# An encoder layer in fp32 on one core: another order at the two heads of the second feed-forward part, norm sums by eight products of ones, norm factors of phase one in PSUM

## The chip, the cores and the metric

The kernel runs on one core of one Trainium2 chip. The metric is the time of one launch in device microseconds (us), the median of several runs; lower is better. The engines are TensorE (PE; its weight loads are PEld), VectorE (DVE), ScalarE (ACT) and GpSimd (POOL); SyncE (SP) issues the DMAs. Each engine works through its own list of instructions in program order, and semaphores tie the lists together.

## The reference

One layer over 1024 + 512 = 1536 token columns with D = 1024, in fp32: a feed-forward part, a mixing part with two kinds of attention heads, a second feed-forward part, a norm at the end. The change touches the end of the mixing part and the second feed-forward part:

```python
def rmsnorm(x, g):
    y = xf * lax.rsqrt(jnp.mean(xf * xf, axis=-1, keepdims=True) + EPS)
    return (y * g).astype(x.dtype)

def swiglu(h, wg, wu, wd):
    return (jax.nn.silu(h @ wg) * (h @ wu)) @ wd
...
x = x + g2 * token_mixing(h, ...)              # ends in  concat(oa, ob) @ w_out
h = modulate(rmsnorm(x, ffn2_norm), sh3, sc3)  # h * (1 + sc3) + sh3
x = x + 0.5 * g3 * swiglu(h, ffn2_wg, ffn2_wu, ffn2_wd)   # D_FF = 2816
x = rmsnorm(x, final_norm)
```

## The kernel before

**Three products for one.** Weights and activations are split into a high and a low half; a product is three products on PE (`three_pass`). ACT copies the high half of a weight tile (`W_hi`), POOL subtracts it from the tile and so makes the low half (`W_lo`). W_hi and W_lo have three slots (WS).

**Output projection** (`wo_*`, L2092 to L2210). The columns are cut into NWC = 4 chunks of NB = 384, and each of the 32 steps (chunk c, row block m) multiplies 8 k-blocks by 3 products, 24 in all, into one of the PSUM banks 0 to 3; DVE adds the result to the state `XT`. The sum of squares over the 1024 rows, which the norm of the next part wants, is made per chunk: ACT squares 8 row blocks (`sums_act`, L737), four slots at a time; POOL adds them in pairs (`pair_up`, L755); PE multiplies each pair sum by a matrix of ones into bank 6 (`sums_pe`, L767), two products (a half, at m = 7) and later two more (at m = 3 of the next chunk). A product of fp32 operands with ones stands in the trace as two matmuls. Then ACT takes the root (`root_act`), DVE the reciprocal (`root_dve`): the norm factor, kept in `rstd_a` (chunks 0, 1: phase one) and `rstd_b` (chunks 2, 3: phase two). The pair sums of chunk 3 are not made before the second part has begun.

**Second feed-forward part** (`st_*`, L2332 to L2712). It works in two phases h = 0, 1 of 768 columns each, with NR = 11 rounds per phase, so 22 rounds R (round 0 is the first of phase one, round 11 the first of phase two; rounds 10 and 21 are each phase's last). A round makes the gate and up products of 256 hidden rows by a scheme of seven products instead of eight for a 2 x 2 block product: PN = 7 products with the names B11, B21, T1, T2, T3, T4, B22, made in this order (`st_product`, L2647), each of 24 matmuls. Then 16 steps of the down product (`st_down`, L2676), 6 matmuls each. The seven weight units and the two down tiles of a round are units u = 0 to 8. Their sources are four quarters of the weights (`quart`), of which POOL makes sums and differences in place (`st_sum`, no = 0 to 3; unit 2 is `qsum`).

**The operands of the seven products** are the normed activations and their differences. Per phase and operand: DVE multiplies state, gain and norm factor (`op_x_dve`, L2279; four row blocks, in one or two pieces), ACT adds the shift (`op_shift_act`), DVE makes the differences T1 to T4 (`op_t_dve`), ACT copies the high half (`op_hi_act`), DVE subtracts for the low part (`op_lo_dve`). For phase one this stands in the projection's last two chunks and the head of round 0; for phase two in rounds 10 and 11.

**Inside a round** ACT copies products out of PSUM (`part_keep_act`), DVE adds them to the next ones (`st_add_dve`), ACT and DVE make the hidden values in four pieces (`st_silu_act`, `st_hidden_dve`, `st_hid_act`, n = 0 to 3). The down product's step 6 waits for the last hidden piece; its steps from the ninth on wait for the additions into the state (`st_down_dve`), of which DVE must have done all but seven. ACT's first split of the next round, `st_hi_act(R, 0, 1)`, stands at the end of its round. SP loads two quarters for the next round behind unit 5's low half and two behind unit 8's.

The order of all this is written out by hand, one function per engine: `st_act` (L2505), `st_dve` (L2598), `st_pool` (L2439), `st_pe` (L2703), and `wo_act`, `wo_pool`, `wo_pe`, `wo_dve` for the projection.

## Time and profile before

| | |
|---|---|
| median of 3 runs | 3147.92 us (3145.74 to 3148.78) |
| the profiled execution | 3152.61 us, its span 3150.7 us, mean granted clock 0.983 |
| busy, whole span | PE 3020.5 us (96%), DVE 1667.9, POOL 1361.6, ACT 1193.6 |
| in the chain that ended last | PE 40%, POOL 9% (of it 8% in attention), issue 6%, DVE 4%, ACT 2% |
| output projection | about 1940 to 2076 us |
| second feed-forward part | 2076 to about 3136 us, then the final norm |

How to read it: the profile is of one execution; a line number is that of the kernel. In a timeline a row is a start, a duration (of the whole group, where it says x2 or more), the engine, line and operation, output<-input, and in brackets the engine's idle time before it with what ended it. The granted clock is a share of PE's full clock: 1.00 is 2.4 GHz, 0.50 is 1.2 GHz.

### The profile page before, as it was taken

The numbers are of one execution on the slowest core, as the hardware profiler recorded it, in microseconds if no ns is written. First come the engines' busy times: TensorE is split into PE (matmuls) and PEld (weight loads), VectorE is DVE, ScalarE is ACT, GpSimd is POOL, SyncE is SP. The second block draws the span as 40 slices with busy tenths as digits, with TensorE's granted clock in tenths as the row PEclk, the third lists the DMA queues.
The fourth block names the chain that finished last, engine by engine and source line by source line (L and its number), as shares of the span: only waits on it lengthen the run. The fifth ranks groups of instructions, "written<-read, shape, count | busy, mean of one in ns | idle before, by whom it ended". The sixth has DMA issues, their size and how long they took to land.

```text
span 3150.7 us, 45626 instructions
## 1 busy us (share of the span) xinstructions
PE 3020.5 (96%) x15385; PEld 2608.0 (83%) x15385; DVE 1667.9 (53%) x3010; ACT 1193.6 (38%) x2026; POOL 1361.6 (43%) x765
## 2 busy tenths in 40 slices
PE   7999999999999988997989999989999998999998
PEld 3888888888888867885656667979999998999998
DVE  5576667766672346886544332353433456434435
ACT  6311111111111135775767775443333343333334
POOL 0111111111111143333646666666666666666673
PEclk9999999999999999998999999989999999999999
DMA  7121212212121023556413225422222121222222
GB/s 268 39 69 52 65 55 80 68 52 63 57 75 34 27 81 119 146 141 163 121 54 83 74 77 160 119 74 67 67 80 67 60 74 41 81 67 67 67 80 100
DMA packets 341520, 262.50 MB, mean 83 GB/s; under 512 B 19771, under 2 KB 309934, under 8 KB 341422
## 3 DMA queue, kind: packets, MB, share of 16 engines
q1 hardware_dynamic: 341422, 261.21, 28.2%
q8 instruction: 59, 0.97, 0.1%
q14 instruction: 39, 0.32, 0.0%
HBM read 215.71 MB, written 45.45 MB: 83 GB/s over the span
## 4 chain that ended last, share of the span: by engine, by line
PE 40%; POOL 9%; issue 6%; DVE 4%; ACT 2%; SPq 1%; DMA 0%; DVEq 0%; POOLq 0%; ACTq 0%
POOL XT_r L1967 8%; PE PS L2671 6%; PE PS L2672 6%; PE PS L2673 6%; PE PS L518 6%; PE PS L519 6%; PE PS L520 6%; POOL W_lo L2416 0%; DVE SL L2327 0%; PE PS L1666 0%; DVE XT L2177 0%; ACT SLf L2303 0%; PE PS L772 0%; ACT z_sb L1184 0%; POOL W_lo L2116 0%
## 5 line engine op out<-in xcount | busy, mean ns | idle before, releaser
L512 POOL TENSOR_TENSOR W_lo<-raw,W_hi 128x1024 fp32r<-128x1024 f32 x66 | 158.7, 2411 | 959.0 <-ACT W_hi L480 959.0
L518 PE MATMUL PS<-H_hi,W_hi 128*128 128x512 f32 (+1 forms) x1312 | 500.3, 381 | 1.9 <-DVE H_lo L1921 1.4
L519 PE MATMUL PS<-H_lo,W_hi 128*128 128x512 f32 (+1 forms) x1312 | 497.0, 379 | 0.0
L520 PE MATMUL PS<-H_hi,W_lo 128*128 128x512 f32 (+1 forms) x1312 | 496.9, 379 | 0.0
L2416 POOL TENSOR_TENSOR W_lo<-quart,W_hi 128x1024 fp32r<-128x1024 f32 x132 | 320.4, 2436 | 263.5 <-ACT W_hi L2412 263.5
L2671 PE MATMUL PS<-SL,W_hi 128*128 128x384 f32 x1056 | 356.6, 338 | 20.8 <-POOL W_lo L2416 19.8
L1967 POOL TENSOR_TENSOR XT_r<-XT,XT_r 128x512 fp32r<-128x512 f32 x224 | 287.0, 1287 | 181.7 <-ACT XT_r L1819 181.1
L2672 PE MATMUL PS<-SL,W_hi 128*128 128x384 f32 x1056 | 355.4, 337 | 0.0
L2673 PE MATMUL PS<-SL,W_lo 128*128 128x384 f32 x1056 | 355.0, 336 | 0.0
L2177 DVE SCALAR_TENSOR_TENSOR XT<-PS,mod,XT 128x384 f32<-128x384 f32 (+1 forms) x480 | 243.2, 534 | 186.2 <-PE PS L520 186.2
L480 ACT ACTIVATE W_hi<-raw 128x1024 fp32r<-128x1024 f32 x66 | 68.6, 1055 | 604.2 <-PE PS L520 604.2
L496 DVE SCALAR_TENSOR_TENSOR ada_acc<-ada_r,silu_c,ada_acc 128x128 f32<-128x128 f32 x672 | 290.4, 473 | 11.9
L518 PEld LDWEIGHTS PS<-H_hi,W_hi 128*128 128x128 f32 x1312 | 246.8, 188 | 45.1 <-DVE H_lo L1921 1.6
L2412 ACT ACTIVATE W_hi<-quart 128x1024 fp32r<-128x1024 f32 x132 | 139.7, 1059 | 376.5 <-PE PS L520 252.1
L519 PEld LDWEIGHTS PS<-H_lo,W_hi 128*128 128x128 f32 x1312 | 246.9, 188 | 41.4
L520 PEld LDWEIGHTS PS<-H_hi,W_lo 128*128 128x128 f32 x1312 | 246.7, 188 | 41.5
L680 DVE SCALAR_TENSOR_TENSOR XT<-PS,mod,XT 128x512 f32<-128x512 f32 x264 | 197.3, 749 | 155.7 <-PE PS L520 155.6
L518 PE MATMUL PS<-hid,W_hi 128*128 128x384 f32 x704 | 237.4, 337 | 6.1 <-POOL W_lo L2416 5.3
L519 PE MATMUL PS<-hid,W_hi 128*128 128x384 f32 x704 | 236.3, 336 | 0.0
L520 PE MATMUL PS<-hid,W_lo 128*128 128x384 f32 x704 | 236.3, 336 | 0.0
L2671 PEld LDWEIGHTS PS<-SL,W_hi 128*128 128x128 f32 x1056 | 200.3, 190 | 22.9 <-POOL W_lo L2416 21.1
L518 PE MATMUL PS<-hid_hi,W_hi 128*128 128x512 f32 x528 | 209.3, 396 | 5.5 <-DVE XT L680 4.9
(294 smaller groups left out, 6291.0 us busy)
## 6 DMA issues: line engine op xcount, KB each, us to landing
ada_r<-in_ada_w SPq DMA_DIRECT2D x192, 128.0 KB, 2.3
quart<-in_ffn_wg SPq DMA_DIRECT2D x88, 256.0 KB, 3.9
quart<-in_ffn_wu SPq DMA_DIRECT2D x88, 256.0 KB, 4.1
down<-in_ffn_wd SPq DMA_DIRECT2D x44, 512.0 KB, 3.5
raw<-in_w_out SPq DMA_DIRECT2D x30, 512.0 KB, 3.7
ada_w_sb<-in_ada_w SPq DMA_DIRECT2D x6, 2048.0 KB, 15.8
raw<-in_ffn_wg SPq DMA_DIRECT2D x22, 512.0 KB, 4.1
raw<-in_ffn_wu SPq DMA_DIRECT2D x22, 512.0 KB, 4.5
```

What stands on the lines that cost most here:

```text
L496: mm = dve.scalar_tensor_tensor(out=acc_, in0=w, scalar=c, in1=acc_, op0=ALU.mult, op1=ALU.add)
L512: pool.tensor_tensor(W_lo[:, n % WS, :], raw[:, n % RS, :], W_hi[:, n % WS, :].bitcast(F32), ALU.subtract).then_inc(w_ready, 1)
L518: pe.matmul(out, w_hi, m_hi, start=first, stop=False)
L519: pe.matmul(out, w_hi, m_lo, start=False, stop=False)
L520: return pe.matmul(out, w_lo, m_hi, start=False, stop=last)
L680: dve.scalar_tensor_tensor(out=xt, in0=PS[:, 6 + i % DS, :], scalar=hgate[:, g, m, c:c + 1], in1=xt, op0=ALU.mult, op1=ALU.add).then_inc(a ...
L1967: pool.tensor_tensor(p_lo(i), e_slot(i), p_hi(i).bitcast(F32), ALU.subtract).then_inc(p_lo_done, 1)
L2177: mm = dve.scalar_tensor_tensor(out=xt, in0=PS[:, bank, a - c * NB:b - c * NB], scalar=hgate[:, g, m, s:s + 1], in1=xt, op0=ALU.mult, op1= ...
L2416: pool.tensor_tensor(W_lo[:, st_slot(u), :], unit_src(u), W_hi[:, st_slot(u), :].bitcast(F32), ALU.subtract) \
L2671: pe.matmul(out, w_hi, m_hi, start=j in PRODUCT_OPENS and kp == 0, stop=False, skip_group_check=True)
L2672: pe.matmul(out, w_hi, m_lo, start=False, stop=False, skip_group_check=True)
L2673: mm = pe.matmul(out, w_lo, m_hi, start=False, stop=kp == 3, skip_group_check=True)
```

## The change

It has three parts. First, the norm sums before the second feed-forward part (b = 2) multiply each of the eight squares by ones, where they multiplied four pair sums; POOL's pair adds are gone, 12 in the projection and 4 in round 0. Second, the norm factors of phase one (chunks 0 and 1) are kept in PSUM banks 4 and 5, not in SBUF (`rstd_a`). Third, the hand-written orders at the heads of both phases change: ACT splits the first three weight units before the operand copies T3, T4, B22; POOL makes unit 2's low half before the difference no = 2; the sums of chunk 3 stand behind T2 and T3, not behind B21 and T1; its root and reciprocals later. For phase two, B11's multiplies and shifts go from round 10 into round 0 (in a free home of their own, rows 12 to 15 of the chunk named EDGE), its high and low copies into the first half of round 10, and the other operands are reordered in rounds 10 and 11, with the first split of round 11 in front of hidden piece 3.

The diff, context cut:

```diff
                 c = i - 2 * NCH
-                return (rstd_a, rstd_b)[c // 2][:, c % 2, :]
+                return PS[:, 4 + c, 0:NB] if c < 2 else rstd_b[:, c % 2, :]
             return rstd_m[:, c * CH:(c + 1) * CH] if i // NCH == 1 else rstd[:, c, :]
...
             for p in range(NPP) if half is None else range(2 * half, 2 * half + 2):
+                if b == 2:
+                    pe.wait_ge(sq_ready, i * KD + 2 * p + 2)
+                    pe.matmul(sum_bank(b), ones[:, :], sq_slot(i, 2 * p), start=(p == 0), stop=False)
+                    pe.matmul(sum_bank(b), ones[:, :], sq_slot(i, 2 * p + 1), start=False,
+                              stop=(p == NPP - 1)).then_inc(sq_used, 1)
+                    continue
                 pe.wait_ge(sq_paired, i * NPP + p + 1)
...
                 wo_split_lo(pool, i)
-                if i % KD == 6 and i // KD < NWC - 1:
-                    pair_up(pool, 2, i // KD, 0)
-                if i % KD == 2 and i > KD:
-                    pair_up(pool, 2, i // KD - 1, 1)
 
...
         RAW_NO = {B11: 0, B21: 4, B12: 8, B22: 13}
-        SHIFT_NO = {B11: 0, B21: 4, B12: 8, B22: 12}
+        SHIFT_NO = ({B11: 0, B21: 4, B12: 8, B22: 12}, {B11: 0, B12: 4, B22: 8, B21: 12})
         OP_T = {T1: (T3, B11), T2: (B22, T1), T4: (B21, T2), T3: (B22, T3)}
...
 
-        def raw_row(j, kp):
+        EDGE = NWC - 1
+        def raw_row(h, j, kp):
             kb, nb = RAW_AT[j]
-            return SLf[:, KD * kb + 4 + kp, nb, :]
+            return SLf[:, 12 + kp, EDGE, :] if h == 1 and j == B11 else SLf[:, KD * kb + 4 + kp, nb, :]
+        def raw4(h, j):
+            return SLf[:, 12:16, EDGE, :] if h == 1 and j == B11 else operand4(SLf, X4f, j, 1)
 
...
             c = 2 * h + nb
-            dve.wait_ge(rstd_ready, 2 * NCH + (2 if h == 0 and nb == 0 else 3 if h == 0 else NWC + 1) - 1)
+            dve.wait_ge(rstd_ready, 2 * NCH + 2 * h + nb + 1)
             if h == 0:
                 dve.wait_ge(wo_done, (1 + nb) * KD)
+            elif j == B11:
+                dve.wait_ge(sq_used, 2 + (2 * NCH + NWC) * NPP)
             else:
...
                     cut = slice(a - c * NB, b - c * NB)
-                    mm = dve.scalar_tensor_tensor(out=raw_row(j, kp)[:, cut], in0=XT[:, k, a:b], scalar=hscale[:, 2, k, s:s + 1],
-                                                  in1=(rstd_a, rstd_b)[h][:, nb, cut], op0=ALU.mult, op1=ALU.mult)
+                    mm = dve.scalar_tensor_tensor(out=raw_row(h, j, kp)[:, cut], in0=XT[:, k, a:b], scalar=hscale[:, 2, k, s:s + 1],
+                                                  in1=(PS[:, 4 + nb, cut] if h == 0 else rstd_b[:, nb, cut]), op0=ALU.mult, op1=ALU.mult)
                 mm.then_inc(op_x, 1)
...
                 for a, b, s in column_spans(c * NB, (c + 1) * NB):
-                    row = raw_row(j, kp)[:, a - c * NB:b - c * NB]
+                    row = raw_row(h, j, kp)[:, a - c * NB:b - c * NB]
                     mm = act.activation(row, row, ACT.Identity, bias=mod[:, SH3 * KD + 4 * kb + kp, s:s + 1])
...
         def op_t_dve(dve, h, j):
-            dve.wait_ge(op_shift, h * 2 * KD + {T1: 12, T2: 16, T4: 16, T3: 16}[j])
+            dve.wait_ge(op_shift, h * 2 * KD + {T1: 12 - 4 * h, T2: 16 - 4 * h, T4: 16, T3: 16 - 4 * h}[j])
             if j != T1:
...
             a, b = OP_T[j]
-            dve.tensor_tensor(operand4(SLf, X4f, j, 1), operand4(SLf, X4f, a, 1), operand4(SLf, X4f, b, 1), ALU.subtract) \
+            dve.tensor_tensor(operand4(SLf, X4f, j, 1), raw4(h, a), raw4(h, b), ALU.subtract) \
                .then_inc(op_x, 1)
...
             else:
-                act.wait_ge(op_shift, h * 2 * KD + SHIFT_NO[j] + 4)
-            act.activation(operand4(SL, X4, j, 0), operand4(SLf, X4f, j, 1), ACT.Copy).then_inc(op_hi, 1)
+                act.wait_ge(op_shift, h * 2 * KD + SHIFT_NO[h][j] + 4)
+            if h == 1 and j == B11:
+                act.wait_ge(st_steps, st_at(NR - 1, product_step(B11, 1)))
+            act.activation(operand4(SL, X4, j, 0), raw4(h, j), ACT.Copy).then_inc(op_hi, 1)
 
         def op_lo_dve(dve, h, j):
-            dve.wait_ge(op_hi, OPH0 + h * PN + j + 1)
-            dve.tensor_tensor(operand4(SL, X4, j, 1), operand4(SLf, X4f, j, 1), operand4(SL, X4, j, 0).bitcast(F32), ALU.subtract) \
+            dve.wait_ge(op_hi, OPH0 + h * PN + (T1 if h == 1 and j == B21 else j) + 1)
+            dve.tensor_tensor(operand4(SL, X4, j, 1), raw4(h, j), operand4(SL, X4, j, 0).bitcast(F32), ALU.subtract) \
                .then_inc(op_ready, 1)
...
                     src = io["ffn2_wd"][0][bass.ds((R * 2 + (t - 2 * h * NR)) * P, P), :]
-                    sp.wait_ge(unit_ready, unit_at(R, 3 + t))
+                    sp.wait_ge(unit_ready, unit_at(R, 4 if is_round(R, 0) else 3 + t))
                     sp.dma_start((down0, down1)[t][:, :], src).then_inc(down_landed[t], 16)
...
             def body(R, h):
-                for u in (2,) if is_round(R, 0) else (1, 2):
-                    st_lo_pool(pool, R, u)
+                if not is_round(R, 0):
+                    st_lo_pool(pool, R, 1)
+                st_lo_pool(pool, R, 2)
                 if is_round(R, 0):
-                    pair_up(pool, 2, NWC - 1)
+                    st_sum(pool, 0, 2)
                 st_sum(pool, R, 3)
...
             st_lo_pool(pool, 0, 1)
-            for no in range(3):
+            for no in range(2):
                 st_sum(pool, 0, no)
...
         DOWN_BANKS = (6, 7, 0, 1, 2, 3, 4, 5)
-        EDGE = NWC - 1
         HOME_1, HOME_E = 8, 10
...
             def body(R, h):
+                turns = is_round(R, NR - 1)
                 if not is_round(R, 0):
                     st_hi_act(act, R, 1)
-                st_hi_act(act, R, 2)
+                    st_hi_act(act, R, 2)
                 if is_round(R, NR):
-                    for j in (T2, T3, T4, B22):
-                        op_hi_act(act, 1, j)
+                    op_hi_act(act, 1, T2)
                 part_keep_act(act, R, 0)
                 part_keep_act(act, R, 1)
+                if is_round(R, 0):
+                    op_hi_act(act, 0, T4)
                 st_hi_act(act, R, 3)
+                if is_round(R, NR):
+                    for j in (T3, T4, B22):
+                        op_hi_act(act, 1, j)
                 if is_round(R, 0):
+                    op_hi_act(act, 0, B22)
                     sums_act(act, 2, NWC - 1, (0, 4))
...
                     sums_act(act, 2, NWC - 1, (4, KD))
+                if turns:
+                    op_hi_act(act, 1, B11)
                 st_hi_act(act, R, 5)
-                if is_round(R, 0):
-                    root_act(act, 2, NWC - 1)
                 part_keep_act(act, R, 2)
                 part_keep_act(act, R, 3)
-                if is_round(R, NR - 1):
-                    op_shift_act(act, 1, B11)
                 st_hi_act(act, R, 6)
...
                 part_keep_act(act, R, 5)
-                if is_round(R, NR - 1):
-                    op_shift_act(act, 1, B21)
-                    op_hi_act(act, 1, B11)
+                if is_round(R, 0):
+                    root_act(act, 2, NWC - 1)
                 st_hi_act(act, R, 7)
...
                 st_silu_act(act, R, 2)
-                if is_round(R, NR - 1):
-                    op_shift_act(act, 1, B12)
                 st_hi_act(act, R, 8)
                 st_hid_act(act, R, 2)
-                if is_round(R, NR - 1):
-                    op_hi_act(act, 1, B21)
+                if turns:
+                    op_shift_act(act, 1, B12)
+                    st_hi_act(act, R, 0, 1)
                 st_silu_act(act, R, 3)
                 st_hid_act(act, R, 3)
-                if is_round(R, NR - 1):
+                if is_round(R, 0):
+                    op_shift_act(act, 1, B11)
+                if turns:
                     op_hi_act(act, 1, T1)
                     op_shift_act(act, 1, B22)
-                if not is_round(R, 2 * NR - 1):
+                    op_shift_act(act, 1, B21)
+                    op_hi_act(act, 1, B21)
+                elif not is_round(R, 2 * NR - 1):
                     st_hi_act(act, R, 0, 1)
 
-            st_hi_act(act, 0, 0)
+            for u in range(WS):
+                st_hi_act(act, 0, u)
             op_hi_act(act, 0, T3)
-            op_hi_act(act, 0, T4)
-            st_hi_act(act, 0, 1)
-            op_hi_act(act, 0, B22)
             st_rounds(act, body)
...
                 if turns:
-                    op_x_dve(dve, 1, B11)
+                    op_lo_dve(dve, 1, B11)
                     op_x_dve(dve, 1, B21)
-                if is_round(R, 0):
-                    root_dve(dve, 2, NWC - 2)
-                    root_dve(dve, 2, NWC - 1)
                 st_add_dve(dve, R, 1)
...
                 st_hidden_dve(dve, R, 1)
+                st_hidden_dve(dve, R, 2)
                 if turns:
                     op_x_dve(dve, 1, B12)
-                st_hidden_dve(dve, R, 2)
-                if turns:
-                    op_t_dve(dve, 1, T1)
                 st_add_dve(dve, R, 3)
...
                 if turns:
+                    op_t_dve(dve, 1, T1)
+                if is_round(R, 0):
+                    root_dve(dve, 2, NWC - 2)
+                    root_dve(dve, 2, NWC - 1)
+                if turns:
                     op_x_dve(dve, 1, B22)
...
                     st_down_dve(dve, R, h, i)
+                    if is_round(R, 0) and i == 7:
+                        op_x_dve(dve, 1, B11)
                     if turns:
                         if i == 3:
-                            op_lo_dve(dve, 1, B11)
-                        if i == 6:
                             op_t_dve(dve, 1, T2)
-                        if i == 9:
+                        if i == 7:
                             op_t_dve(dve, 1, T4)
-                        if i == 12:
+                        if i == 11:
                             op_lo_dve(dve, 1, B21)
...
                     st_product(pe, R, h, j)
-                    if is_round(R, 0) and j in (B21, T1):
-                        sums_pe(pe, 2, NWC - 1, j - B21)
+                    if is_round(R, 0) and j in (T2, T3):
+                        sums_pe(pe, 2, NWC - 1, j - T2)
                 st_down(pe, R, h)
...
```

Three places on ACT show the order. The first is the head of the second feed-forward part. `W_hi<-quart` and `W_hi<-qsum` are weight splits, `SL<-SLf` and `X<-X4f` high copies of operands, `SLf<-PS` copies of products, `SLf<-XT` squares. Before:

```order
L2412 ACTIVATE W_hi<-quart 128x1024
L2323 ACTIVATE SL<-SLf 128x4x384
L2323 ACTIVATE X<-X4f 128x1536
L2412 ACTIVATE W_hi<-quart 128x1024
L2323 ACTIVATE SL<-SLf 128x4x384
L2412 ACTIVATE W_hi<-qsum 128x1024
L2492 ACTIVATE SLf<-PS 128x384 x2
L2412 ACTIVATE W_hi<-quart 128x1024
```

After:

```order
L2423 ACTIVATE W_hi<-quart 128x1024 x2
L2423 ACTIVATE W_hi<-qsum 128x1024
L2334 ACTIVATE SL<-SLf 128x4x384
L2503 ACTIVATE SLf<-PS 128x384 x2
L2334 ACTIVATE X<-X4f 128x1536
L2423 ACTIVATE W_hi<-quart 128x1024
L2334 ACTIVATE SL<-SLf 128x4x384
L753 ACTIVATE SLf<-XT 128x384 x4
```

The three splits stand together now, ahead of the copies of T3 (first `SL<-SLf`), T4 (`X<-X4f`) and B22.

The second is ACT's list from the split of the last down tile to the end of round 0. Before:

```order
L2412 ACTIVATE W_hi<-down 128x1024
L2503 ACTIVATE hid<-PS 128x384
L2499 ACTIVATE hid_g<-PS 128x384
L2503 ACTIVATE hid<-PS 128x384
L2412 ACTIVATE W_hi<-quart 128x1024
```

After:

```order
L2423 ACTIVATE W_hi<-down 128x1024
L2514 ACTIVATE hid<-PS 128x384
L2510 ACTIVATE hid_g<-PS 128x384
L2514 ACTIVATE hid<-PS 128x384
L2312 ACTIVATE SLf<-SLf,mod 128x256
L2312 ACTIVATE SLf<-SLf,mod 128x128
...
L2423 ACTIVATE W_hi<-quart 128x1024
```

Eight shifts of phase two's B11 (four rows in pieces of 256 and 128 columns) have moved in front of round 1's first split.

The third is the end of round 10 and the start of round 11. Before:

```order
L2323 ACTIVATE SL<-SLf 128x4x384
L2303 ACTIVATE SLf<-SLf,mod 128x384 x4
L2412 ACTIVATE W_hi<-quart 128x1024 x2
L2412 ACTIVATE W_hi<-qsum 128x1024
L2323 ACTIVATE SL<-SLf 128x4x384 x2
L2323 ACTIVATE X<-X4f 128x1536
L2323 ACTIVATE SL<-SLf 128x4x384
L2492 ACTIVATE SLf<-PS 128x384 x2
L2412 ACTIVATE W_hi<-quart 128x1024 x2
L2499 ACTIVATE hid_g<-PS 128x384
```

After:

```order
L2334 ACTIVATE SL<-SLf 128x4x384
L2423 ACTIVATE W_hi<-quart 128x1024
L2423 ACTIVATE W_hi<-qsum 128x1024
L2334 ACTIVATE SL<-SLf 128x4x384
L2503 ACTIVATE SLf<-PS 128x384 x2
L2423 ACTIVATE W_hi<-quart 128x1024
L2334 ACTIVATE SL<-SLf 128x4x384
L2334 ACTIVATE X<-X4f 128x1536
L2334 ACTIVATE SL<-SLf 128x4x384
L2423 ACTIVATE W_hi<-quart 128x1024
L2510 ACTIVATE hid_g<-PS 128x384
```

The first split of round 11 has left this place (it stands further ahead, before hidden piece 3), T2's copy stands alone in front of the product copies, and the copies of T3, T4 and B22 behind the next split.

## Rows read from the trace of the kernel before

**Rows 1.** Windows: busy time per engine (instructions), granted clock, DMA share, GB/s.

```profile
1975.00:2025.00 50.00, 50.00 (x280) 48.40 (x279) 16.47 (x23) 21.26 (x29) 30.17 (x16) 1.00 0.36 106
...
2076.00:2123.00 47.00, 32.74 (x148) 30.05 (x147) 18.64 (x15) 22.67 (x31) 31.71 (x15) 0.82 0.16 49
2123.00:2169.00 46.00, 46.00 (x266) 45.72 (x265) 17.76 (x30) 16.23 (x25) 30.87 (x14) 1.00 0.24 70
```

**Rows 2.** PE's waits in the whole span: us in total, times, longest.

```profile
PE PS L2671 <- POOL W_lo L2416: 19.8, 3, 9.7
...
PE PS L518 <- POOL W_lo L2416: 5.3, 1, 5.3
```

**Rows 3.** Timeline of PE: start, us, operation, idle before it and its releaser.

```profile
2088.66 0.69 PE L2671 MATMUL PS<-SL,W_hi 128*128 128x384 f32 x1 [8.21 <-POOL W_lo L2416]
...
2099.26 0.56 PE L772 MATMUL PS<-SLf,ones 128*128 128x384 f32 x1 [4.08 <-POOL SLf L759]
...
2110.02 0.50 PE L2671 MATMUL PS<-SL,W_hi 128*128 128x384 f32 x1 [1.98 <-POOL W_lo L2416]
...
2592.60 0.66 PE L518 MATMUL PS<-hid,W_hi 128*128 128x384 f32 x1 [5.34 <-POOL W_lo L2416]
...
2635.71 0.69 PE L2671 MATMUL PS<-SL,W_hi 128*128 128x384 f32 x1 [9.65 <-POOL W_lo L2416]
```

**Rows 4.** Windows of 2 us, PE alone: busy (matmuls), granted clock.

```profile
2090.00:2092.00 2.00, 2.00 (x7) 0.50 0.00 0
```

**Rows 5.** Timeline of ACT: the split that waits for a round's last product.

```profile
2145.44 1.06 ACT L2412 ACTIVATE W_hi<-quart 128x1024 fp32r<-128x1024 f32 x1 [11.06 <-PE PS L520]
...
2557.36 1.06 ACT L2412 ACTIVATE W_hi<-quart 128x1024 fp32r<-128x1024 f32 x1 [12.14 <-PE PS L520]
...
2612.25 1.06 ACT L2412 ACTIVATE W_hi<-quart 128x1024 fp32r<-128x1024 f32 x1 [11.66 <-PE PS L520]
...
2670.97 1.06 ACT L2412 ACTIVATE W_hi<-quart 128x1024 fp32r<-128x1024 f32 x1 [12.28 <-PE PS L520]
```

**Rows 6.** Timeline of PE: starts of two following halves of products of ones.

```profile
2039.52 0.81 PE L772 MATMUL PS<-x_sqo,ones 128*128 128x384 f32 x2
...
2057.46 0.81 PE L772 MATMUL PS<-x_sqo,ones 128*128 128x384 f32 x2
```

**Rows 7.** Timeline of DVE: four multiplies by a norm factor, POOL busy and idle.

```profile
2055.70 4.33 DVE L2292 SCALAR_TENSOR_TENSOR SLf<-XT,mod,rstd_a 128x384 f32<-128x384 f32 x4
...
2596.75 2.20 DVE L2292 SCALAR_TENSOR_TENSOR SLf<-XT,mod,rstd_b 128x384 f32<-128x384 f32 x4
```

**Rows 8.** Timelines of POOL and DVE at the projection's end.

```profile
2063.96 7.57 POOL L2116 TENSOR_TENSOR W_lo<-raw,W_hi 128x1024 fp32r<-128x1024 f32 x2 [5.94 <-ACT W_hi L2112]
...
2065.49 3.78 DVE L2315 TENSOR_TENSOR X4f<-SLf 128x1536 f32<-128x1536 f32 x1
...
2069.72 7.30 DVE L2327 TENSOR_TENSOR SL<-SLf,SL 128x1536 fp32r<-128x1536 f32 x2
...
2083.00 1.74 DVE L2327 TENSOR_TENSOR X<-X4f,X 128x1536 fp32r<-128x1536 f32 x1
```

**Rows 9.** Timelines round the end of round 0, and multiplies for phase two.

```profile
2109.84 2.55 DVE L779 RECIPROCAL rstd_b<-rstd_b 128x384 f32<-128x384 f32 x1 [4.33 <-ACT rstd_b L764]
...
2125.99 2.40 POOL L2416 TENSOR_TENSOR W_lo<-down,W_hi 128x1024 fp32r<-128x1024 f32 x1 [1.87 <-ACT W_hi L2412]
...
2130.81 1.72 DVE L2177 SCALAR_TENSOR_TENSOR XT<-PS,mod,XT 128x384 f32<-128x384 f32 x3
...
2133.31 1.06 ACT L2412 ACTIVATE W_hi<-quart 128x1024 fp32r<-128x1024 f32 x1 [3.01 <-DMA quart<-in_ffn_wu]
...
2573.59 2.71 DVE L2292 SCALAR_TENSOR_TENSOR SLf<-XT,mod,rstd_b 128x256 f32<-128x256 f32 x8
```

**Rows 10.** Timelines of DVE and ACT in round 11.

```profile
2633.37 0.96 DVE L2567 TENSOR_TENSOR PS<-PS,SLf 128x768 f32<-128x768 f32 x1
...
2635.49 0.49 ACT L2503 ACTIVATE hid<-PS 128x384 fp32r<-128x384 f32 x1 [0.63 <-DVE PS L2587]
```


## The prediction

> **What bounds the kernel now.** I read the windows first: in the output projection (first row of [rows 1]) PE is busy 50.00 of 50 us at full clock, and so it is in an ordinary round. Only the stretch behind 2076 is thin: 32.74 of 47 us, mean clock 0.82. So PE sets the time, and the other engines count only where PE waits. The list of waits says for whom: POOL's low halves of weights, 19.8 us in three waits and 5.3 in one [rows 2]. PE's timeline places them [rows 3]: 8.21, 4.08 and 1.98 us in round 0 (the middle one for the pair adds), 5.34 and 9.65 in rounds 10 and 11. Behind each the clock is at its lower level for a while (0.50, so 1.2 GHz, 7 matmuls in 2 us where full clock has 12 [rows 4]), which costs some 2 us a time. ACT's first weight split of a round waits for PE's last product of the round before and marks the rounds [rows 5]: round 1 begins at 2145.4, round 10 at 2557.3 (45.8 us each), round 12 at 2670.9. Round 0 begins at 2076.0: 24 products at 0.173 us (46 us hold 266, [rows 1]) and 8.2 idle before 2088.66. So round 0 takes 69.4 us, where 45.8 and 2.6 for its norm sums would do: 21 too many. Rounds 10 and 11 take 113.6 against 91.5: 22 too many. These 43 us are all that an order can win.
>
> **Part one: eight products of ones.** Two logical products stand in the trace as x4. From one half's start to the next are 17.94 us [rows 6], and between them lie 96 weight products, 16.64 us; so a half costs 1.30. The change gives each half four instead of two: +1.30 for each of six halves in the output projection, where PE is never idle: +7.8 us on the path. POOL's pair adds that go there cost nothing (POOL waits for ACT, ACT for PE). The two halves of round 0 move and grow to 2.6 each; they are in the walk below.
>
> **Part two: norm factors in PSUM.** Four multiplies by a norm factor take 4.33 us while POOL works and 2.20 while it doesn't [rows 7]: the waiting one lets a POOL operation pass. The same holds for other DVE work with both inputs in SBUF [rows 8]: two splits on POOL take 7.57 us instead of 2 x 2.39, the subtraction between them on DVE 3.78 instead of 1.74, two more 7.30. The two engines take turns, one operation each. With the factor in PSUM one SBUF input is left, and 4.33 should become about 2.3. This is worth 0: the shift behind it on ACT waits for the root, and that for PE's sums. The Trainium skill ("SBUF — State Buffer", Who interferes with whom) says that a VectorE instruction with two SBUF inputs contends with a GpSimd one that reads SBUF, and that one with a single SBUF input doesn't; by this rule, the trace agrees. The same rule speaks against the next part, whose subtractions now stand where POOL has a queue.
>
> **Part three, round 0.** Times from the end of the projection (2076.0 before), each step a wait and a duration: split on ACT 1.06, on POOL 2.39, DVE subtraction 1.7, turns as above. Up to the first low half nothing changes its place: POOL ends it at -0.6, DVE then takes its turn (T1's low part) to 1.0, and the second low half is there at 3.4 instead of 12.6. B21 runs from 4.2 to 8.3, no wait: 8.2 saved. But POOL now has a sum, a difference and the third low half in a row, and DVE's operations take turns with them: T3's subtraction to 5.05, POOL's sum to 7.4, T2's low part to 9.05, the difference to 11.4, T3's low part (its copy comes off ACT at 9.9) to 13.05, the low half to 15.4. The product T1 waits 7.1 us for it. Then T4's low part to 17.05, two more differences to 21.8 and the fourth low half: T2 at 24.2 (before at 34.0, with 2.6 of sums in front). T2 runs at the lower clock to 30.4, sums to 33.0. The second four squares on ACT wait for these sums, and behind them on ACT stand a weight split and the copy of T2's product, for which T3 waits: squares to 33.9, split 35.0, copy 35.5. T3 starts 2.5 us late. Then T3, sums, T4, B22 at 4.16, 2.6, 4.16, 4.16 and about 2 for the clock: the down products start at 52.7. Before: 2145.4 less 16.6 is 2128.8, also 52.7. Worth 0, between -8 (POOL and DVE don't hinder each other: T1 at 9.0, T2 at 16.2, down at 44.7) and +2.
>
> **End of round 0.** From the start of the down products: DVE ends the hidden part at 2.1, then two reciprocals of 2.55 [rows 9] that stood earlier before, to 7.2, eight additions at 0.55 [rows 9] to 11.6, then the eight multiplies for phase two's B11, 2.7 to 3.3 with POOL waiting (2.71 in [rows 9]), to 14.9. ACT shifts the last at 15.6, and only then splits the first quarter of round 1: 16.7, where it did so at 4.5 before (2133.31 in [rows 9], waiting for its DMA). POOL's low half stands at 19.1, and PE wants it at 16.6: 2.5 late. Behind it on POOL are two sums and the next low half: 26.3, where B11 of round 1 ends at 23.3: 3.0 more. Round 1 loses 5.5; the lower clock behind the first gap stretches B11 inside the second. Bounds 3 and 8.
>
> **Rounds 10 and 11.** From round 10's start. B11's multiplies are gone from it, so DVE gives the sums for B22 at 23.6, PE needs them at 25.0; the last low half stands at 28.6, the down products start at 29.1 instead of 35.3: 5.9 saved. But DVE's multiplies for B12 start at 27.3 and let a POOL sum pass (to 33.2); the quarter for round 11 lands 4.9 us behind the last low half (2128.4 to 2133.3 in [rows 9]), at 33.5; ACT splits it to 34.8 and then does hidden 3, done at 37.0, which PE wants at 35.4: 1.7. Then DVE does T1's subtraction and B22's multiplies, and three POOL operations pass between them, to 45.8, before the first addition of the down products; PE stands at its ninth product from 39.1 to 46.4: 7.3. Eight more m's of 1.04 and 2 for the clock end the round at 57.0; before at 54.9 (2612.25 in [rows 5]). In round 11 the weight of T2 doesn't wait for four copies on ACT any more: T2 at 72.6 instead of 78.4. But DVE's addition in B21's banks stands behind five low parts and a subtraction, each with a turn of POOL's: at 79.9, before at 76.1 [rows 10]. Hidden 0 is through ACT 2.6 us behind the addition's start [rows 10], then come a split (1.06) and the copy of T2's product (0.49): 84.0. T3 waits for this copy. Before, T3 started at 84.6 (78.4, a product and 2 for the clock), the copies following PE at once. Worth 0, between -13 (no turns: 71) and +3.
>
> **Sum.** 7.8 + 0 + 5.5 + 0 = 13.3 us. The profiled execution took 3152.6, so 3165.9 by the profiler's run; it lies 4.7 above the median of 3147.9, so 3161 as median.
>
> **Rivals.** *It gains by part (a).* The order does what its words say and POOL and DVE hinder each other less than in rows 8, since the instructions meet at other moments: -8 in round 0, +5.5, -11 in rounds 10 and 11, +7.8: 6 us faster, 3142. For it: turns depend on arrivals within a microsecond. Against: in rows 8 each meeting costs a full operation. *It gains fully (b).* Every wait gone: -43 + 7.8 + 2.6, 3115. Against: four chains above would all have to be wrong. The other side of my forecast is (a): the point from which it decides is T1 in round 0 at 12 or earlier and T3 in round 11 at 75 or earlier. *Only the PE work counts (c).* The hold on round 1's first quarter is hidden, since DVE catches up sooner: 7.8 + 0 + 1, and 4 won in round 11 because T2 is earlier: 5 slower, 3153. Against: the hold is in ACT's program order, not in a race. *Slower still (d).* Turns also hit round 1 and T4, and clock losses add up: +20 to +24, 3170.
>
> **How the numbers follow.** Forecast 0.48, (a) 0.16, (b) 0.04, (c) 0.20, (d) 0.12. The likeliest case alone spans 3155 to 3168. The range for 8 in 10 reaches from just above (a), 3144, to 3171. A change below 0.2% (6.3 us) can't be told from none here. Faster by more: (b) and 0.10 of (a), 0.14. Same: 0.06 of (a), 0.14 of (c), 0.04 of the forecast: 0.24. Slower: 0.62.
>
> **What would show it.** x_sqo products 48 instead of 24, the projection 7.8 longer from its first to its last product. In round 0 a PE wait for the third low half near 7 us, a short one at T3 for ACT's copy. In round 1 ACT's first quarter split about 12 us later than before behind the down start, and PE waits of 2 to 3 us at B11 and B21. In round 10 a PE wait of about 7 for DVE's addition in the down products, in round 11 one before T3 for ACT's copy. I am wrong if round 1 starts without a wait, if rounds 10 and 11 together fall under 105 us, or if POOL's splits beside DVE's subtractions take 2.4.

## The result, and the profile after

The changed kernel takes 3158.54 us (median of 7 runs, 3154.91 to 3160.34), the kernel before 3148.78 beside it (3144.64 to 3151.79): ratio 1.0029, 95% interval 1.002 to 1.0038. It is 9.8 us slower, or 0.3%, and the interval doesn't reach 1. Its profiled execution took 3157.36 us, with a span of 3155.5 us at a mean clock of 0.984.

I read it by stages and not by its total, since the stages ahead of the change end at other moments in each execution: ACT's first weight split of the output projection that waits for PE stands at 1938.89 us before and at 1935.17 after, in code that is the same. ACT's splits that wait for PE's last product mark the rounds (start, us, operation, idle before it and its releaser). Before, beside [rows 5]:

```profile
1938.89 1.06 ACT L2112 ACTIVATE W_hi<-raw 128x1024 fp32r<-128x1024 f32 x1 [5.94 <-PE PS L520]
...
2191.20 1.06 ACT L2412 ACTIVATE W_hi<-quart 128x1024 fp32r<-128x1024 f32 x1 [12.07 <-PE PS L520]
```

The same marks after: the projection's first split, then the start of rounds 1, 2, 10, 11 and 12.

```profile
1935.17 1.06 ACT L2118 ACTIVATE W_hi<-raw 128x1024 fp32r<-128x1024 f32 x1 [6.94 <-PE PS L520]
...
2145.36 1.06 ACT L2423 ACTIVATE W_hi<-quart 128x1024 fp32r<-128x1024 f32 x1 [1.09 <-PE PS L520]
...
2197.57 1.06 ACT L2423 ACTIVATE W_hi<-quart 128x1024 fp32r<-128x1024 f32 x1 [11.67 <-PE PS L520]
...
2563.70 1.06 ACT L2423 ACTIVATE W_hi<-quart 128x1024 fp32r<-128x1024 f32 x1 [12.15 <-PE PS L520]
...
2619.41 1.06 ACT L2423 ACTIVATE W_hi<-quart 128x1024 fp32r<-128x1024 f32 x1 [6.18 <-PE PS L520]
...
2677.28 1.06 ACT L2423 ACTIVATE W_hi<-quart 128x1024 fp32r<-128x1024 f32 x1 [12.14 <-PE PS L520]
```

PE's short wait for the projection's last weight but one divides the projection from its end and round 0; before, and after:

```profile
2067.70 0.45 PE L518 MATMUL PS<-H_hi,W_hi 128*128 128x384 f32 x1 [0.46 <-POOL W_lo L2116]
```

```profile
2071.74 0.44 PE L518 MATMUL PS<-H_hi,W_hi 128*128 128x384 f32 x1 [0.46 <-POOL W_lo L2122]
```

The differences of these marks, in us, in the trace of one execution each:

| stage | before | after | change |
|---|---|---|---|
| projection, to the wait of 0.46 | 128.81 | 136.57 | +7.76 |
| its last two weights, and round 0 | 77.74 | 73.62 | -4.12 |
| round 1 | 45.76 | 52.21 | +6.45 |
| rounds 2 to 9 | 366.16 | 366.13 | 0 |
| round 10 | 54.89 | 55.71 | +0.82 |
| round 11 | 58.72 | 57.87 | -0.85 |
| sum | 732.08 | 742.11 | +10.03 |

Behind round 11 both take 473.5 us to the last operation on DVE. The two profiled executions differ by 4.8 us only, since the part ahead of the first mark was 3.7 us shorter in the second, in code that is the same, and its end behind DVE's last operation 1.5. So I put the 9.8 us of the medians down to these stages: the ones products, less what round 0 won, and a loss in round 1. Round 0's and round 1's numbers are those of one execution; other executions of the same order differ by up to 3.2 and 1.6 us (table below, last section).

PE's timeline after shows where it waits (start, us, operation, idle and releaser; the rows that answer to [rows 3]):

```profile
2094.88 0.69 PE L2686 MATMUL PS<-SL,W_hi 128*128 128x384 f32 x1 [6.22 <-POOL W_lo L2427]
...
2103.52 0.44 PE L2686 MATMUL PS<-SL,W_hi 128*128 128x384 f32 x1 [1.44 <-POOL W_lo L2427]
...
2113.06 0.41 PE L2686 MATMUL PS<-SL,W_hi 128*128 128x384 f32 x1 [2.50 <-ACT SLf L2503]
...
2147.11 0.44 PE L2686 MATMUL PS<-SL,W_hi 128*128 128x384 f32 x1 [1.79 <-POOL W_lo L2427]
...
2154.05 0.44 PE L2686 MATMUL PS<-SL,W_hi 128*128 128x384 f32 x1 [2.51 <-POOL W_lo L2427]
...
2600.08 0.44 PE L518 MATMUL PS<-hid,W_hi 128*128 128x384 f32 x1 [1.11 <-DVE hid L2604]
...
2608.88 0.69 PE L518 MATMUL PS<-hid,W_hi 128*128 128x384 f32 x1 [6.44 <-DVE XT L2179]
...
2634.58 0.44 PE L2686 MATMUL PS<-SL,W_hi 128*128 128x384 f32 x1 [2.79 <-POOL W_lo L2427]
...
2645.64 0.66 PE L2686 MATMUL PS<-SL,W_hi 128*128 128x384 f32 x1 [6.60 <-ACT SLf L2503]
```

These are T1, T2 and T3 of round 0, B11 and B21 of round 1, the down products of round 10 (two rows), and T2 and T3 of round 11. Of the five long waits of before three are gone (8.21, 4.08 and 5.34), and T2's two are shorter: 1.44 for 1.98 in round 0, 2.79 for 9.65 in round 11. Seven others are new. Together PE now waits 31.4 us in these rounds, and 30.8 before (the five and two of under 1 us). The releasers name the engine: POOL at T1, T2, B11 and B21, ACT at T3, DVE at the down products. Whether program order is behind them is what the experiments show.

Why POOL is late in round 0 stands in the timelines of POOL and DVE after, which answer to [rows 8]:

```profile
2075.51 7.79 POOL L2427 TENSOR_TENSOR W_lo<-quart,W_hi 128x1024 fp32r<-128x1024 f32 x2
2083.27 3.91 POOL L2448 TENSOR_TENSOR qsum<-quart 128x1024 f32<-128x1024 f32 x1
2087.26 3.75 POOL L2448 TENSOR_TENSOR quart<-quart 128x1024 f32<-128x1024 f32 x1
2090.98 3.85 POOL L2427 TENSOR_TENSOR W_lo<-qsum,W_hi 128x1024 fp32r<-128x1024 f32 x1
2094.79 3.88 POOL L2448 TENSOR_TENSOR quart<-qsum,quart 128x1024 f32<-128x1024 f32 x1
2098.75 2.38 POOL L2448 TENSOR_TENSOR quart<-quart 128x1024 f32<-128x1024 f32 x1
```

```profile
2085.37 3.43 DVE L2338 TENSOR_TENSOR SL<-SLf,SL 128x1536 fp32r<-128x1536 f32 x1
2089.68 2.95 DVE L2338 TENSOR_TENSOR SL<-SLf,SL 128x1536 fp32r<-128x1536 f32 x1 [0.88 <-ACT SL L2334]
2092.56 3.89 DVE L2338 TENSOR_TENSOR X<-X4f,X 128x1536 fp32r<-128x1536 f32 x1
```

Up to 2098.7 each POOL operation that takes 2.38 alone takes 3.75 to 3.91; with no subtraction on DVE beside it, it is 2.38 again. The three that end with T1's low half (at 2094.8) are longer by 1.4 to 1.5 us each.

### The profile page after: what moved, and what is told of

Read it like the earlier page. It is cut to its first block, busy times and chain, and to the rows that moved or that the text cites. A ratio compares the mean times of both kernels' runs of the same rounds, so it can differ in the third digit from the quotient of the medians.

```text
span 3155.5 us, 45675 instructions
## 1 busy us (share of the span) xinstructions
PE 3027.6 (96%) x15417; PEld 2616.1 (83%) x15417; DVE 1673.2 (53%) x3010; ACT 1194.3 (38%) x2026; POOL 1349.3 (43%) x749
## 4 chain that ended last, share of the span: by engine, by line
PE 40%; POOL 9%; issue 6%; DVE 4%; ACT 1%; SPq 1%; DMA 0%; DVEq 0%; POOLq 0%; ACTq 0%
POOL XT_r L1973 8%; PE PS L2686 6%; PE PS L2688 6%; PE PS L2687 6%; PE PS L518 6%; PE PS L519 6%; PE PS L520 6%; POOL W_lo L2427 0%; DVE SL L2338 0%; DVE XT L2179 0%; PE PS L774 0%; PE PS L773 0%; PE PS L1672 0%; ACT z_sb L1190 0%; DVE SLf L2324 0%
```

## The experiments

Each median is of 5 to 11 runs, which spread over 3.5 to 10 us. The kernel before had medians of 3147.9 to 3149.0 us beside them. Edits are to the changed kernel unless the text says otherwise. The last five columns are stage lengths as above; "proj" is the projection, "0" its last two weights with round 0. They are those of one execution each. A stage in which PE doesn't wait repeats to 0.02 us; one in which it does varies with the clock (last section): the changed order's round 10 took 55.3 to 56.7 us, and its round 11 57.6 to 58.3.

| version | median | ratio to before (interval) | proj | 0 | 1 | 10 | 11 |
|---|---|---|---|---|---|---|---|
| before | 3148.8 | | 128.81 | 77.74 | 45.76 | 54.89 | 58.72 |
| changed | 3158.5 | 1.0029 (1.002, 1.0038) | 136.57 | 73.62 | 52.21 | 55.71 | 57.87 |
| pair sums back | 3152.3 | 1.0008 (0.9999, 1.0017) | 128.81 | 73.59 | 50.62 | 55.33 | 57.63 |
| before, with products | 3154.6 | 1.0026 (1.0016, 1.0037) | 136.57 | 76.17 | 45.77 | 53.53 | 59.69 |
| split first | 3154.6 | 1.0016 (1.0007, 1.0025) | 136.58 | 75.20 | 45.76 | 55.79 | 57.89 |
| spread | 3155.4 | 1.0017 (1.0008, 1.0026) | 136.58 | 75.22 | 50.63 | 52.09 | 59.48 |
| copies first | 3157.1 | 1.0028 (1.0018, 1.0039) | 136.58 | 76.77 | 50.59 | 56.70 | 55.07 |
| low parts late | 3158.0 | 1.003 (1.0018, 1.0042) | 136.57 | 72.22 | 51.98 | 56.51 | 58.30 |
| squares late | 3156.9 | 1.0032 (1.002, 1.0044) | 136.57 | 70.87 | 51.92 | 56.49 | 58.29 |
| factors in SBUF | 3159.0 | 1.0029 (1.0018, 1.004) | 136.58 | 73.62 | 52.21 | 55.73 | 57.85 |
| four edits | 3140.1 | 0.9972 (0.996, 0.9983) | 128.81 | 73.61 | 45.76 | 109.20 | (both) |
| six edits | 3135.7 | 0.9959 (0.9945, 0.9972) | 128.82 | 67.89 | 45.76 | 52.11 | 56.77 |
| eight edits | 3134.3 | 0.9953 (0.994, 0.9967) | 128.81 | 67.87 | 45.77 | 109.08 | (both) |
| eight, T3 first | 3134.9 | 0.9959 (0.9945, 0.9972) | 128.81 | 67.90 | 45.76 | 108.26 | (both) |

**Pair sums back on POOL in the projection.**

```
-                if b == 2:
+                if b == 2 and c == NWC - 1:      # eight products of ones only in round 0
...
                 wo_split_lo(pool, i)
+                if i % KD == 6 and i // KD < NWC - 1:
+                    pair_up(pool, 2, i // KD, 0)
+                if i % KD == 2 and i > KD:
+                    pair_up(pool, 2, i // KD - 1, 1)
```

> The changed kernel with the pair sums put back on POOL for the five column groups whose norm sums run inside the output projection; round 0's sums stay eight products of ones. My theory (each product of ones is on the path, since PE never waits in the projection): the projection is 7.7 us shorter again and nothing else moves, so 3158.5 less 7.7 is 3151, and this part alone explains most of the 9.8 us between the two kernels. Rival 1 (POOL's and DVE's turns: the pair adds cost DVE enough that its additions free the banks late, so the pair adds were not free): under 4 us gained, 3155 or more. Rival 2 (what is won in the projection is lost in round 0, whose waits for POOL grow by as much): 3158.

The median falls by 6.3 us, and the projection takes 128.81 us, to the hundredth what it takes before. Both rivals fall: the adds cost PE nothing, and T1's wait in round 0 stays at 6.22. (The column groups are three, the chunks 0 to 2 with six halves; the expectation says five by mistake.)

**The kernel before, with the products alone.** The same edit the other way round, in the old order.

```
+                if b == 2 and c < NWC - 1:
+                    ...  # two products of ones per pair, no wait for the pair adds
...
-                if i % KD == 6 and i // KD < NWC - 1:
-                    pair_up(pool, 2, i // KD, 0)
-                if i % KD == 2 and i > KD:
-                    pair_up(pool, 2, i // KD - 1, 1)
```

> The kernel before with one part of the change alone: in the projection eight products of ones per column group and no pair adds; round 0 and all later rounds in the old order. My theory: the projection takes 7.76 us more (128.81 to 136.57 from ACT's first split to PE's wait at the last weight but one), the rest keeps its length: 3148.9 plus 7.8, 3156.7. Rival (POOL, free of the pair adds, ends its last weights of the projection earlier and takes 1 to 2 us from round 0's 8.2 us wait): 3155.

The projection takes 136.57 us, again as in the changed kernel; the median rises by 6.7. Round 0's first wait is 8.18 us as before (8.21 in [rows 3]), so POOL's relief wins nothing there and the rival falls. The stage itself is 1.6 us shorter: behind T2's wait the clock stayed at 1.00 here, where it was 0.57 in the kernel before (2110 to 2114).

**Norm factors back in SBUF.**

```
-                return PS[:, 4 + c, 0:NB] if c < 2 else rstd_b[:, c % 2, :]
+                return (rstd_a, rstd_b)[c // 2][:, c % 2, :]
```

> The changed kernel with the norm factors of phase one back in SBUF. My theory (the multiplies take turns with POOL again, 4.3 us for four instead of 2.2, but they stand off the path): the projection and round 0 keep their lengths, 3158.5 within 2. Rival 1 (they delay the low parts and subtractions behind them, which meet POOL's queue in round 0 later and worse): T1's wait grows by 1 to 4 us, 3160 to 3162. Rival 2 (a later start of DVE's tail leaves POOL undisturbed at first): 2 us faster.

Every stage has the length of the changed kernel's within 0.02 us, and T1 waits 6.20. Yet the multiplies themselves change as expected. In the changed kernel, and in this one (DVE's timeline, four multiplies each, POOL busy on a weight beside both):

```profile
2058.44 2.18 DVE L2301 SCALAR_TENSOR_TENSOR SLf<-XT,mod,PS 128x384 f32<-128x384 f32 x4
```

```profile
2062.94 4.33 DVE L2301 SCALAR_TENSOR_TENSOR SLf<-XT,mod,rstd_a 128x384 f32<-128x384 f32 x4
```

2.15 us a time are won on DVE and nothing on the path.

**ACT's split of round 1's first quarter first.**

```
                 if is_round(R, 0):
+                    st_hi_act(act, R, 0, 1)
                     op_shift_act(act, 1, B11)
...
-                elif not is_round(R, 2 * NR - 1):
+                elif not is_round(R, 0) and not is_round(R, 2 * NR - 1):
                     st_hi_act(act, R, 0, 1)
```

> The changed kernel with ACT's split of round 1's first weight quarter ahead of the four shifts of phase two's first operand block at the end of round 0. My theory (round 1's two waits, 1.8 and 2.5 us in the trace of the changed kernel, and the low clock behind them come from this split standing behind shifts that wait for DVE): ACT splits some 9 us earlier, both waits go, 6 us are won, 3152. Rival (POOL's queue or the DMA of the quarter ends next: the low half is still late, or it meets DVE's multiplies in turns, each of which then costs more): one wait of 1 to 3 us stays, 2 to 3 us won, 3156. If nothing is won the waits had another cause.

The median falls by 4.0 us (the traces say 4.9 for rounds 0 and 1 together). Round 1 starts and goes without a wait, in 45.76 us as before. ACT's timeline of this kernel shows what the order had held:

```profile
2134.20 1.06 ACT L2423 ACTIVATE W_hi<-quart 128x1024 fp32r<-128x1024 f32 x1 [2.12 <-DMA quart<-in_ffn_wu]
2143.16 2.88 ACT L2312 ACTIVATE SLf<-SLf,mod 128x256 f32<-128x256 f32 x8 [7.89 <-DVE SLf L2301]
```

The split waits for its DMA alone and is done at 2135.3; the shifts behind it wait 7.89 us for DVE. Those were ahead of it.

**The phase-two operations spread over the down products of round 10.**

```
-                    op_t_dve(dve, 1, T1)                 # ahead of the additions
-                    op_x_dve(dve, 1, B22)
...
                     if turns:
+                        if i == 0:
+                            op_t_dve(dve, 1, T1)
+                        if 1 <= i <= 4:
+                            op_x_dve(dve, 1, B22, (i - 1,))
-                        if i == 3:                       # T2, T4, B21: 3, 7, 11
+                        if i == 6:                       # T2, T4, B21: 6, 9, 12
```

> The changed kernel with DVE's subtraction for T1 and its four multiplies for B22 of phase two taken out from in front of the down products' additions in round 10 and put between them, one behind each of the first five additions (the next two subtractions and the low part follow at the 7th, 10th and 13th). My theory (PE's 6.4 us at the ninth down product are these five DVE operations, each with a turn of POOL's, in front of the first addition): that wait falls to under 1 us; T2's low part is needed only at the third product of round 11, so up to 8 us are won with the clock, 3151. Rival 1 (the DVE work is only moved: it now holds the last additions, or round 11's first operands come later, and round 11 waits longer for what round 10 wins): 3157 to 3159. Rival 2 (half: one operation between two additions is 2.7 to 4.4 us with POOL beside it where PE takes 1.04 a product, so the banks run out later, at the 13th product, by 3 us): 3155.

The wait of 6.44 us becomes three of 1.43, 1.35 and, at B11 of round 11, 1.11 us. DVE's program order was the cause of the larger part; that POOL's turns on the operations between two additions make what is left is my reading, which no run tried. Round 10 is 3.6 us shorter, round 11 1.6 longer, where T3 waits 7.75 us for ACT's copy instead of 6.60. The median falls by 3.1: half of my theory, half of the first rival.

**The copies of T2's product first in round 11.**

```
+                if is_round(R, NR):
+                    part_keep_act(act, R, 2)
+                    part_keep_act(act, R, 3)
                 st_silu_act(act, R, 0)
...
-                part_keep_act(act, R, 2)
-                part_keep_act(act, R, 3)
+                if not is_round(R, NR):
+                    part_keep_act(act, R, 2)
+                    part_keep_act(act, R, 3)
```

> The changed kernel with ACT's two copies of T2's product in round 11 ahead of the first silu, which waits for DVE's addition. My theory (T3 waits 6.6 us because these copies stand behind a silu, a hidden copy and a weight split that all wait for DVE's late addition): T3's wait falls to what its weight or its operand's low part needs; T2 ends at about 2641.6 in the trace of the changed kernel and the addition there starts at 2641.6, so T3 could start 4 to 5 us earlier, and 5 us are won, 3153.5. Rival (the next in the chain is as late: the split of T4's weight and the addition in B21's banks move behind, B22 or the down products wait instead for the hidden parts): the wait moves to T4 or the down products, 3157 to 3160.

Round 11 is 2.8 us shorter; the median moves by 1.5 only, less than these medians tell apart. The copy no longer ends a wait, but POOL's queue does, at T3 and T4 (PE's timeline of this kernel):

```profile
2638.78 0.44 PE L2690 MATMUL PS<-SL,W_hi 128*128 128x384 f32 x1 [2.96 <-POOL W_lo L2427]
...
2650.16 0.44 PE L2690 MATMUL PS<-X,W_hi 128*128 128x384 f32 x1 [2.77 <-POOL W_lo L2427]
```

**DVE's low parts of T3, T4 and B22 late in round 0.**

```
-            for j in (T2, T3, T4, B22):
-                op_lo_dve(dve, 0, j)
+            op_lo_dve(dve, 0, T2)
...
                 st_hidden_dve(dve, R, 0)
+                if is_round(R, 0):
+                    for j in (T3, T4, B22):
+                        op_lo_dve(dve, 0, j)
```

> The changed kernel with DVE's low parts of T3, T4 and B22 of phase one taken from the end of the projection to behind the first hidden part of round 0; T2's stays. In the changed kernel POOL's operations take 3.4 to 3.9 us each from 2068 to 2098.7 and 2.38 behind that, where DVE's low parts have ended. My theory (POOL's lateness in round 0 is DVE's turns): from 2087 on POOL's operations take 2.4, so the third low half is 2.8 us earlier (PE's wait at T1 6.2 to 3.4), the fourth some 4 us earlier, and the rest of round 0 with it: 3 to 4 us won, 3155. Rival 1 (POOL's durations there are its own, whatever DVE does): no gain, T1's wait stays at 6.2. Rival 2 (the low parts come too late, since they now stand behind ACT's silu and copy: T3 waits for its low part): T1's wait falls, T3's grows, 3158 to 3161.

POOL's timeline of this kernel (compare the six rows above; its times run 1.9 us later):

```profile
2085.16 3.90 POOL L2447 TENSOR_TENSOR qsum<-quart 128x1024 f32<-128x1024 f32 x1
2089.14 3.76 POOL L2447 TENSOR_TENSOR quart<-quart 128x1024 f32<-128x1024 f32 x1
2092.85 2.34 POOL L2426 TENSOR_TENSOR W_lo<-qsum,W_hi 128x1024 fp32r<-128x1024 f32 x1
2095.16 2.36 POOL L2447 TENSOR_TENSOR quart<-qsum,quart 128x1024 f32<-128x1024 f32 x1
```

With no DVE operation to take turns with, the same low half takes 2.34 us instead of 3.85 and the next difference 2.36 instead of 3.88. T1's wait falls to 4.72, not to 3.4, since T2's low part still meets two operations; T3 starts 3.0 us earlier. So rival 1 is refuted by the durations. Of the 3 us the stage keeps 1.4: behind T3's wait the clock was lower here (0.64 from 2112 to 2116), where it stayed at 1.00 in the changed kernel; such a fall costs 1.6 us (last section). The median shows nothing (0.5 us).

**ACT's second squares of round 0 behind the copies.**

```
-                if is_round(R, 0):
-                    sums_act(act, 2, NWC - 1, (4, KD))
...
                 part_keep_act(act, R, 3)
+                if is_round(R, 0):
+                    sums_act(act, 2, NWC - 1, (4, KD))
```

> The changed kernel with ACT's second four squares of round 0 behind the two copies of T2's product instead of in front of the weight split before them. My theory (T3's 2.5 us wait in round 0 are these squares, which wait for PE's first sums, ahead of the copy): the wait goes, 2.5 us are won and no clock, 3156. Rival (the second sums then wait for the squares behind T3, since ACT does them late): the same comes back as a wait of PE's sums, 3158.

T3's wait is gone, and the second sums don't wait: the stage is 2.75 us shorter. The median fell by 1.7 us, which alone would not show it.

**The edits together.** Four: pair sums back, split first, spread, copies first. Six: with low parts late and squares late. Eight: with this for round 11 (low parts late there too, T3's weight ahead of the copies):

```
                 if is_round(R, NR):
+                    st_hi_act(act, R, 4)
                     for j in (T3, T4, B22):
                         op_hi_act(act, 1, j)
...
-                    for j in (T3, T4, B22):
-                        op_lo_dve(dve, 1, j)
                 st_add_dve(dve, R, 0)
                 st_hidden_dve(dve, R, 0)
-                if is_round(R, 0):
+                if is_round(R, h * NR):
                     for j in (T3, T4, B22):
-                        op_lo_dve(dve, 0, j)
+                        op_lo_dve(dve, h, j)
```

> The changed kernel with all four edits of the first group together: pair sums back in the projection, ACT's split first at the end of round 0, the phase-two operations spread over the down products of round 10, and T2's copies ahead of the silu in round 11. If the four act by themselves their single gains add up (6.3, 4.0, 3.1 and 1.5 by the medians): 3143.6, 5 us under the kernel before. My theory: the last two help each other, since what the spread won in round 10 (3.6 us) was given back half at T3's wait for the copy (7.75 us instead of 6.6), which the fourth edit removes: 3141 to 3143. Rival: POOL's queue in round 11 ends both (with the copies moved T3 and T4 waited 2.97 and 2.77 us for it), so together they give no more than the larger of the two: 3145.

> The four edits together (3140.1) and with them the two that act on round 0: DVE's low parts of T3, T4 and B22 behind the first hidden part, and ACT's second squares behind the copies. Alone these two moved the median by 0.5 and 1.7 us, but the traces show T3 3.0 us earlier from the start of round 0 by the one and its 2.5 us wait gone by the other. My theory (both are real and the median of so few runs hides them, since a lower clock behind T1's wait took back part of the first): 4 to 5 us under 3140.1, 3136. Rival (the clock behind a wait takes back what the shorter waits bring, as in the first of them, where round 1 ended only 1.6 us earlier): 1 to 2 us, 3138.5.

> As the six edits together, and in round 11 DVE's low parts of T3, T4 and B22 behind the first hidden part too, and ACT's split of T3's weight ahead of its copies for these three. With the four edits the only long wait left in rounds 10 and 11 is T3's, 4.13 us for POOL's low half, whose split stands behind three copies on ACT (done 2625.5, though its weight was there before 2620). My theory: the split is 7 us earlier, POOL doesn't meet DVE's low parts, and T3 is then held only by its own operand's low part and T2's copy: 2 to 4 us less than the six, 3133. Rival (T3's operand comes late: its subtraction on DVE ends at 2621.3 in the trace of the four edits, then a copy on ACT, then the low part, now behind addition, silu and copy): T3's wait stays 4 us or grows by 1 to 2, same as or 2 us above the six.

The four give 3140.1, 18.4 us under the changed kernel, where their single gains by the medians add up to 14.9. That doesn't show that the copies and the spread help each other: by the stages the single gains add up to 18.0 (7.8 in the projection, 6.4 in round 1, 2.0 and 1.8 in rounds 10 and 11). Rounds 10 and 11 together take 109.2, against 113.6 in the changed kernel and 111.6 and 111.8 with one of the two: 4.4 us less, where 3.8 is their sum, and these stages vary by more than the 0.6 between. What the traces do show is T3's wait, 4.13 us with both edits, 7.75 with the spread alone. The six give 3135.7, as expected; the stage with round 0 is down to 67.9 us from 77.7 before. The eight give 3134.3, which can't be told from the six; their rival was right. PE's timelines at T3 of round 11, in the six and in the eight:

```profile
2625.10 0.69 PE L2697 MATMUL PS<-SL,W_hi 128*128 128x384 f32 x1 [6.03 <-POOL W_lo L2430]
```

```profile
2622.17 0.66 PE L2697 MATMUL PS<-SL,W_hi 128*128 128x384 f32 x1 [5.98 <-DVE SL L2341]
```

The wait stays, with another releaser: the weight was there, but T3's low part stood behind the hidden part, and that behind three copies on ACT. The last version puts T3's own chain first:

```
-                    for j in (T3, T4, B22):
-                        op_hi_act(act, 1, j)
+                    op_hi_act(act, 1, T3)
+                    part_keep_act(act, R, 2)
+                    part_keep_act(act, R, 3)
+                    op_hi_act(act, 1, T4)
+                    op_hi_act(act, 1, B22)
...
                 st_add_dve(dve, R, 0)
+                if is_round(R, NR):
+                    op_lo_dve(dve, 1, T3)
                 st_hidden_dve(dve, R, 0)
```

> As the last of the combined versions, and in round 11 T3's own chain first: ACT's two copies of T2's product directly behind the high part of T3, DVE's low part of T3 directly behind the addition in B21's banks. In the trace before it T3 waited 5.98 us for this low part, which stood behind a silu on ACT that waited 4.56 us behind three copies. My theory: the low part ends at about 2617 to 2618.5 instead of 2622.07, T3's wait falls from 6.0 to 1 to 2 us, and with the clock 4 us are won: 3130.5. Rival (what is won at T3 is lost at T4 or at the down products, whose hidden parts now wait for a later silu): 3133 to 3134.

T3's wait falls to 1.09 us, and T4 then waits 3.79 for POOL; rounds 10 and 11 together win 0.8 us, the median nothing. This rival was right too: the wait moved on to POOL's queue in round 11. Whether another order there would win more, no run tried.

The version with eight edits is faster than both kernels: 14.6 us under the kernel before, 24 under the changed one.

## Why the prediction was right, and which term was off

*Ones products.* 7.8 expected, 7.76 measured, both ways. A half starts at 1964.04 and the next at 1983.27 in PE's timeline after, 19.23 us apart where [rows 6] have 17.94: 1.29 a half, six halves.

```profile
1964.04 0.81 PE L773 MATMUL PS<-x_sqo,ones 128*128 128x384 f32 x2
...
1983.27 0.81 PE L773 MATMUL PS<-x_sqo,ones 128*128 128x384 f32 x2
```

*Norm factors in PSUM.* Four multiplies in 2.18 us instead of 4.33, worth 0: both halves of the step hold, shown by the version with the factors in SBUF.

*Round 0: the mis-sized term.* I had 0, it was -4.1. The walk of POOL's and DVE's turns held: counting from the start of round 0 (8.3 us behind the wait of 0.46), T1 starts at 14.8 (predicted 15.4), T2 at 23.5 (24.2), and T3 waits 2.50 for ACT's copy (2.5). What failed is the clock. "T2 runs at the lower clock to 30.4" and "about 2 for the clock" ahead of the down products together cost 4 us in my sum; in this execution the clock was at its upper level from 2102 on, through the waits of 1.44 and 2.50, so T3 started at 33.0 instead of 35.5 and round 0 ended at 65.3 instead of 69.4. In the execution of the version with the copies first, whose instructions are the same up to round 11, the lower clock came, behind T2's wait and behind T3's. Windows of 4 us, PE alone (busy, matmuls, granted clock, DMA), after:

```profile
2104.00:2108.00 4.00, 4.00 (x24) 1.00 0.75 262
...
2112.00:2116.00 4.00, 2.94 (x17) 1.00 0.00 0
2116.00:2120.00 4.00, 4.00 (x18) 1.00 0.93 261
```

and with the copies first in round 11:

```profile
2104.00:2108.00 4.00, 4.00 (x16) 0.57 0.68 262
...
2112.00:2116.00 4.00, 1.50 (x6) 0.85 0.00 0
2116.00:2120.00 4.00, 4.00 (x19) 0.72 0.55 160
```

There the stage took 76.77 us, 3.15 more than here, where my sum was 4.1 too high. The old order varies too: 77.74 in the kernel before, 76.17 in the version with the products alone, whose round 0 is the same. So the term is a range of -4.1 to +0.6 by the clock alone, and the two executions compared lie at its lower end. My 0 lies inside it, too high against most of its values: I had counted two falls of the clock at 2 us each as sure, where each costs 1.6 and comes in some executions only.

*End of round 0 and round 1.* 5.5 expected, 6.2 to 6.5 in four executions, this one with 6.45 among them, and 4.8 to 4.9 in three others. ACT's split comes at 2143.22, 14.8 us behind the first down product at 2128.44 (predicted 15.6); PE's two waits are 1.79 and 2.51 (2.5 and 3.0). The waits are 1.2 us shorter than I had them, and what carries this execution over 5.5 is the lower clock behind the second one (0.69 from 2154 to 2158), which I had only behind the first. The split put first removes both waits: the cause is ACT's program order, and rival (c), by which this hold would be hidden, falls.

*Rounds 10 and 11.* 0 expected, 0.0 measured. The waits are the ones foreseen: 6.44 at the ninth down product (7.3), 2.79 at T2 and one for the copy at T3, 81.9 us behind the start of round 10 (84.0). That the sum came out to the tenth is luck. Round 10 lost 0.8 us where my walk has 2.1. T3 started at 2641.65 before, 84.3 us behind the start of round 10, so it came 2.4 us earlier and not 0.6. Its product then took 6.5 us instead of 4.2, at a mean clock of 0.63 behind the wait of 6.60, and for this fall my walk has nothing.

*The turns.* The rule of the Trainium skill ("SBUF — State Buffer", Who interferes with whom) that VectorE with two SBUF inputs and GpSimd contend, and with one SBUF input don't, is borne out twice: 3.85 to 2.34 us on POOL when DVE's low parts go, 4.33 to 2.18 on DVE when one input is in PSUM. Rivals (a) and (b) needed T1 at 12 or earlier and T3 of round 11 at 75; they came at 14.8 and 81.9. What round 0 won against my sum is therefore not rival (a), though half of its 8 us came: the turns came as foreseen, and the low clock didn't.

The expected gain of some 43 us behind the projection went so: the wait of 8.2 us for POOL came back as one of 6.2 behind a POOL queue that now stands ahead of T1, in which the turns make each of the last three operations 1.4 to 1.5 us longer (taking DVE away from one of them won 1.5 us of the wait). Three new waits are program order, each shown by moving one piece: squares ahead of a copy (2.5), shifts ahead of a split (4.8 to 6.5 with the clock), multiplies ahead of an addition (6.4, of which the move took 3.6 off round 10).
